# The MLP of a two-layer trunk in four quarters of 1024 hidden units in place of two halves

## What is computed

```
h   = layer_norm(ALPHA * h + mix, ...)
hid = square(relu(h @ mlp_w_up[layer] + mlp_b_up[layer]))        # 1024 -> 4096
h   = layer_norm(ALPHA * h + hid @ mlp_w_down[layer] + mlp_b_down[layer], ...)   # 4096 -> 1024
```

## Time and profile before

| | |
|---|---|
| Median of 3 runs | 1367.02 us (1365.03 to 1369.89) |
| The profiled execution | 1364.11 us, its span 1362.3 us |
| PE busy | 1312.8 us (96% of the span), granted clock 0.995 on average |
| DVE busy | 625.6 us (46%) |
| POOL busy | 515.8 us (38%) |
| ACT busy | 512.1 us (38%) |
| Moved by DMA | 108.27 MB, mean 79 GB/s, queue q1 with 141296 packets at 25.9% of 16 engines |

### The profile page before, as it was taken

One profiled execution on the slowest core, in us unless ns is written; L12 is line 12 of the kernel. 1 busy time (PEld: TensorE's weight loads), 2 busy tenths in 40 slices (PEclk: granted clock), 3 DMA queues, 4 the chain that ended last, 5 costly groups with the idle time before them and its releaser, 6 DMA issues.

```text
span 1362.3 us, 21811 instructions
## 1 busy us (share of the span) xinstructions
PE 1312.8 (96%) x9502; PEld 1178.8 (87%) x9502; DVE 625.6 (46%) x1052; ACT 512.1 (38%) x734; POOL 515.8 (38%) x220
## 2 busy tenths in 40 slices
PE   6999998999999999999999999999999999999996
PEld 5998855999999999999998988877788888888885
DVE  6999554456530024412356456465566300343125
ACT  4334487445222222222365245264453222223124
POOL 1001154355444444445544124114654444444440
PEclk9999999999999999999999999999999999999998
DMA  6221100222233322333221221212223333223321
GB/s 183 93 63 33 64 1 1 69 88 68 90 92 93 93 94 93 94 93 94 94 63 63 63 63 63 62 63 93 93 64 97 106 103 95 93 93 93 93 63 62
DMA packets 141791, 108.27 MB, mean 79 GB/s; under 512 B 8096, under 2 KB 139376, under 8 KB 141696
## 3 DMA queue, kind: packets, MB, share of 16 engines
q1 hardware_dynamic: 141296, 106.77, 25.9%
q10 hardware_dynamic: 400, 0.11, 0.0%
HBM read 104.77 MB, written 2.10 MB: 78 GB/s over the span
## 4 chain that ended last, share of the span: by engine, by line
PE 83%; ACT 7%; DVE 6%; issue 2%; DMA 1%; POOL 1%; SPq 0%; DVEq 0%; ACTq 0%
PE pb L706 63%; PE pb L872 2%; PE pb L718 2%; PE pb L873 2%; PE pb L874 2%; PE pb L812 1%; PE pb L813 1%; PE pb L750 1%; PE pb L811 1%; ACT wh L1289 1%; PE pb L1073 1%; DMA x_tok<-in_x 1%; DVE st L2313 1%; PE pb L982 1%; PE pb L1071 1%
## 5 line engine op out<-in xcount | busy, mean ns | idle before, releaser
L567 POOL TENSOR_TENSOR wl<-raw,wh 128x2048 fp32r<-128x2048 f32 x81 | 378.4, 4672 | 513.3 <-ACT wh L1289 513.1
L706 PE MATMUL pb<-hh,wh 128*128 128x264 f32 (+1 forms) x1160 | 301.6, 318 | 3.2 <-DVE qd L2295 1.6
L706 PE MATMUL pb<-hh,wl 128*128 128x264 f32 (+1 forms) x1160 | 296.9, 314 | 0.0
L706 PE MATMUL pb<-hl,wh 128*128 128x264 f32 (+1 forms) x1160 | 296.8, 314 | 0.0
L1289 ACT ACTIVATE wh<-raw 128x2048 fp32r<-128x2048 f32 x97 | 185.1, 1908 | 92.3 <-DMA raw<-in_mlp_w_down 62.2
L706 PEld LDWEIGHTS pb<-hh,wh 128*128 128x128 f32 x1160 | 190.7, 188 | 19.2 <-issue 3.7
L706 PEld LDWEIGHTS pb<-hl,wh 128*128 128x128 f32 x1160 | 190.6, 188 | 13.8 <-issue 1.2
L706 PEld LDWEIGHTS pb<-hh,wl 128*128 128x128 f32 x1160 | 190.5, 188 | 13.5
L706 PE MATMUL pb<-hidh,wh 128*128 128x264 f32 (+1 forms) x720 | 191.8, 321 | 0.0
L706 PE MATMUL pb<-hidh,wl 128*128 128x264 f32 (+1 forms) x720 | 191.0, 320 | 0.0
L706 PE MATMUL pb<-hidl,wh 128*128 128x264 f32 (+1 forms) x720 | 190.2, 318 | 0.0
(11 more groups left out here) (391 smaller groups left out, 2043.2 us busy)
## 6 DMA issues: line engine op xcount, KB each, us to landing
raw<-in_mlp_w_up SPq DMA_DIRECT2D x32, 1024.0 KB, 5.3
raw<-in_mlp_w_down SPq DMA_DIRECT2D x32, 1024.0 KB, 5.5
raw<-in_w_in_c SPq DMA_DIRECT2D x16, 1024.0 KB, 5.2
raw<-in_w_in_ab SPq DMA_DIRECT2D x8, 1024.0 KB, 5.5
raw<-in_w_out_ab SPq DMA_DIRECT2D x4, 1024.0 KB, 4.9
raw<-in_w_out_c SPq DMA_DIRECT2D x4, 1024.0 KB, 5.0
x_tok<-in_x SPq DMA_DIRECT2D x2, 1024.0 KB, 8.2
raw<-in_s_w_glu SPq DMA_DIRECT2D x1, 1024.0 KB, 5.4
```

The costliest lines, as they stand in the source:

```text
L567: pool.tensor_tensor(wl[:, c % RING, :], raw[:, c % RING, :], wh[:, c % RING, :].bitcast(F32), ALU.subtract).then_inc(w_lo, 1)
L706: mm = pe.matmul(pb[:, bank + b, 0:z_ - a], lhs, rhs[:, a:z_], start=first and hi and k == 0, stop=last and k == len(todo) - 1)
```

## The change

The MLP of each layer is cut in four quarters of 1024 hidden units: `up{l}q` and `down{l}q` with q = 0 to 3, each of 4 slots, 8 tiles, 8 chunks. The slots of the down stages now hold two tiles by 8 chunks, as all others of that size do. `down{l}0` is emptied as before (ACT with the bias, DVE with ALPHA*h), `down{l}3` by the layer norm. `down{l}1` and `down{l}2` are added to `h` by DVE straight from PSUM, one tensor_tensor a tile, and ACT has no part in them but the high parts of four slots, which in its program no longer wait for a tile. `hidh` and `hidl` become half as large. The matmuls are the same in number and size.

```
--- before.py
+++ after.py
@@ -42,9 +42,9 @@
     layer1 = [(f"{w}{p}", 1, n) for p in range(NPAIR) for w, n in (("f", 2), ("q", 2), ("i", NBLK))]
     for name, slots, tiles in [
         ("uqk", 6, 12), ("v", 2, 2 * NBLK), ("glu", 1, 4), ("out_ab", 4, 8),
-        ("up00", 8, 16), ("down00", 8, 8), ("up01", 8, 16), ("down01", 8, 8),
+        *[(f"{w}0{q}", 4, 8) for q in range(4) for w in ("up", "down")],
         *layer1, ("g", 4, 8), ("out_c", 4, 8),
-        ("up10", 8, 16), ("down10", 8, 8), ("up11", 8, 16), ("down11", 8, 8),
+        *[(f"{w}1{q}", 4, 8) for q in range(4) for w in ("up", "down")],
     ]:
         STAGES[name] = (slot, slots, tile, tiles)
         slot += slots
@@ -53,9 +53,9 @@
 
 
 NSLOTS = _plan()
-TOK = {"q0", "q1", "q2", "q3", "g", "out_c", "up10", "down10", "up11", "down11"}
-IN_TMP = ["glu", "up00", "down00", "up01", "up10", "down10", "up11"]
-LN_STAGE = ["out_ab", "down01", "out_c", "down11"]
+TOK = {"q0", "q1", "q2", "q3", "g", "out_c", *[f"{w}1{q}" for q in range(4) for w in ("up", "down")]}
+IN_TMP = ["glu", *[n for l in "01" for n in (f"up{l}0", f"down{l}0", f"up{l}1", f"up{l}2", f"up{l}3")]]
+LN_STAGE = ["out_ab", "down03", "out_c", "down13"]
 LOW_LN = {STAGES[name][0] + STAGES[name][1] + 2: n for n, name in enumerate(LN_STAGE[:3])}
 HALF_OUT = {0: 0, 2: 4}
 PIECES = {(0, 6): (0,), (0, 7): (1,), (1, 2): (2,), (1, 4): (3,)}
@@ -75,7 +75,7 @@
     count, table = {"act": 0, "dve": 0}, []
     for name, (_, _, _, tiles) in STAGES.items():
         for t in range(tiles):
-            by = "dve" if name == "glu" or name[0] in "fq" or name in LN_STAGE else "act"
+            by = "dve" if name == "glu" or name[0] in "fq" or name in LN_STAGE or name[:4] == "down" and name[5] in "12" else "act"
             count[by] += 1
             table.append((by, count[by]))
     return table
@@ -266,8 +266,8 @@
 
 
         m2 = ExitStack()
-        hidh = sb("hidh", [P, 16, LEAD + L], F32R, m2)[:, :, LEAD:]
-        hidl = sb("hidl", [P, 16, LEAD + L], F32R, m2)[:, :, LEAD:]
+        hidh = sb("hidh", [P, 8, LEAD + L], F32R, m2)[:, :, LEAD:]
+        hidl = sb("hidl", [P, 8, LEAD + L], F32R, m2)[:, :, LEAD:]
         rel = sb("rel", [P, 4, L], F32, m2)
         m2.close()
         m3 = ExitStack()
@@ -532,9 +532,9 @@
             stream("out_ab", w_out_ab[0], skip=2)
 
             def mlp(layer):
-                for half in range(2):
-                    stream(f"up{layer}{half}", mlp_w_up[layer], col0=2048 * half)
-                    stream(f"down{layer}{half}", mlp_w_down[layer][2048 * half:2048 * (half + 1), :], P, 16)
+                for q in range(4):
+                    stream(f"up{layer}{q}", mlp_w_up[layer], col0=1024 * q)
+                    stream(f"down{layer}{q}", mlp_w_down[layer][1024 * q:1024 * (q + 1), :])
 
             mlp(0)
             for p in range(NPAIR):
@@ -664,7 +664,7 @@
                                    ALU.subtract).then_inc(y_ready, 1)
             lows("glu")
             lows_ln(0)
-            for name in ["up00", "down00", "up01"]:
+            for name in ["up00", "down00", "up01", "down01", "up02", "down02", "up03"]:
                 lows(name)
             lows_ln(1)
             for p in range(NPAIR):
@@ -680,7 +680,7 @@
             for i in range(8):
                 out_low(i)
             lows_ln(2)
-            for name in ["up10", "down10", "up11"]:
+            for name in ["up10", "down10", "up11", "down11", "up12", "down12", "up13"]:
                 lows(name)
             lows_ln(3)
 
@@ -877,14 +877,14 @@
                             pieces(j * per + k)
 
             def mlp(layer, n):
-                for half in range(2):
-                    if half == 0:
+                for q in range(4):
+                    if q == 0:
                         run_after(n)
                     else:
-                        run(f"up{layer}1", hh, hl)
-                    seen = 16 * (2 * layer + half)
-                    run(f"down{layer}{half}", hidh, hidl, lambda k: (hid_ready, seen + k + 1), cols_=P, kcs=16,
-                        norm=2 * layer + 1 if half else None)
+                        run(f"up{layer}{q}", hh, hl)
+                    seen = 8 * (4 * layer + q)
+                    run(f"down{layer}{q}", hidh, hidl, lambda k: (hid_ready, seen + k + 1),
+                        norm=2 * layer + 1 if q == 3 else None)
 
 
             pe.wait_ge(consts, 3)
@@ -1271,9 +1271,9 @@
                         if kc % 4 == 3:
                             mm.then_inc(ot_done, 1)
                     if a == 0 and kc == 0:
-                        last_sum("down11", 3, 1)
+                        last_sum("down13", 3, 1)
                     if a == 0 and kc == 1:
-                        last_square("down11", 3, 1)
+                        last_square("down13", 3, 1)
 
 
         @block.scalar
@@ -1650,13 +1650,16 @@
             run_ln(0)
 
             def mlp(layer):
-                for half in range(2):
-                    c0 = 64 + 32 * layer + 16 * half
-                    run(f"up{layer}{half}", into_tmp(f"up{layer}{half}", ACT.Relu, lambda t: cols_a[:, c0 + t:c0 + t + 1]),
-                        None if half else lambda t, a: ahead_out(layer, t, a))
-                    if half == 0:
+                for q in range(4):
+                    c0 = 64 + 32 * layer + 8 * q
+                    run(f"up{layer}{q}", into_tmp(f"up{layer}{q}", ACT.Relu, lambda t: cols_a[:, c0 + t:c0 + t + 1]),
+                        None if q else lambda t, a: ahead_out(layer, t, a))
+                    if q == 0:
                         run(f"down{layer}0", into_tmp(f"down{layer}0", ACT.Identity,
                                                       lambda t: cols_b[:, 32 + 8 * layer + t:32 + 8 * layer + t + 1]))
+                    elif q < 3:
+                        for j in range(4):
+                            high(STAGES[f"down{layer}{q}"][0] + j + 2)
                 run_ln(2 * layer + 1)
 
             mlp(0)
@@ -2111,6 +2114,11 @@
 
                 _, _, t0, tiles = STAGES[name]
                 for t in range(tiles):
+                    if name[5] != "0":
+                        hc = cols(name, h[:, t, :])
+                        dve.wait_ge(tile_done, t0 + t + 1)
+                        TT(hc, hc, dense(name, t), ALU.add).then_inc(emptied_by["dve"], 1)
+                        continue
                     hm = flat(name, h[:, t, :])
                     wait_tile(name, t)
                     STT(hm, hm, ALPHA, flat(name, tmp[:, (t0 + t) % 2, :]), ALU.mult, ALU.add).then_inc(tmp_free, 1)
@@ -2224,7 +2232,7 @@
 
                 t0 = STAGES[name][2]
                 freed = 2 + tmp_before(name)
-                for t in range(16):
+                for t in range(8):
                     par = (t0 + t) % 2
                     a = flat(name, tmq[:, par, :])
                     r = flat(name, rel[:, t, :] if name[-1] == "0" and t < 4 else tmp[:, par, :])
@@ -2236,9 +2244,10 @@
                     TT(flat(name, hidl[:, t, :]), a, flat(name, hidh[:, t, :].bitcast(F32)), ALU.subtract).then_inc(hid_ready, 1)
 
             def mlp(layer):
-                hidden(f"up{layer}0")
-                residual(f"down{layer}0")
-                hidden(f"up{layer}1")
+                for q in range(3):
+                    hidden(f"up{layer}{q}")
+                    residual(f"down{layer}{q}")
+                hidden(f"up{layer}3")
                 layer_norm(2 * layer + 1, 1.0)
 
             layer_norm(0, ALPHA)
```

35 lines of the change are left out of this document (20 added, 15 removed).

## The result

| | before | after |
|---|---|---|
| Median | 1367.02 us (13 runs, 1364.1 to 1369.97) | 1370.3 us (13 runs, 1369.35 to 1375.38) |
| The profiled execution, its span | 1364.11, 1362.3 | 1369.84, 1367.9 |
| From norm 0's first add to the end of the span | 1070.8 | 1076.5 |

The ratio is 1.0031, with a 95% interval of 1.002 to 1.0043: slower by 0.3%, at the edge of what a measurement of this kernel can tell. The forecast was 1369.9 us. The two profiled executions stand 5.7 us apart, though, twice the 2.85 of the sum. The medians hide this, since the median of before lies 2.9 us above its profiled execution and that of after only 0.5 above its own. The lowest times, 1364.1 and 1369.35, are 5.25 apart. So the question for the experiments is what the sum left out.

The account below looks back on a forecast made before the run. PE's own matmul pace was taken as the bound, its work unchanged. Norm 1 +1.15, norm 3 +1.94 and pace -0.24 make +2.85 us, on the median of before 1369.9 us (+0.21%); range 1365.0 to 1377.0.

Parts of the forecast that it names:

- the sum: All terms together: norm 1 +1.15, norm 3 +1.94, pace -0.24, the rest 0, giving +2.85 us.
- Loads, high and low parts, evacuations at 0: Body of the MLP: loads, high and low parts and 16 added DVE adds per layer stay hidden behind PE, worth 0.
- Up to down at 0: Up-to-down turns, four a layer: slack before the last hidden chunk shrinks from 7.4 to 1.6 and 1.4 us; worth 0.
- POOL before `hidl`: Rival, end of up stages: POOL's low part blocks DVE, PE stalls 3.1 us a place, +25 for all; chance 0.10.
- Norm 1, +1.15: Norm 1: half 0 ends 2.88 us later, the chain gets 1.73 shorter through L2121 at 0.61; +1.15 us.
- Norm 3, +1.94: Norm 3, end of kernel: half 0 ends 2.80 us later, a 0.86 us wait for half 1 goes; +1.94 us.
- pace, -0.24: Layer 1's slow end behind the guess of the mean holds 60 matmuls less, at 4 ns each; -0.24 us.
- a fall behind norm 1: Rival: PE's clock falls behind norm 1 as behind norm 0, costing 1.33 us, 1371.2 us; chance 0.22.
- The chances: Odds given for the result against before: same 0.61, slower 0.35, faster 0.04, with 4.1 us (0.3%) as the bound.

Follow-up runs that it names:

- p_last16: The changed kernel with three parts a layer, of 8, 8 and 16 chunks, so the last stage is a half again; 1364.9 us, 0.9997 of before.
- a_race: The changed kernel with ACT's high part ahead of the ReLU at the last tile of every up stage; 1444.27 us, 1.0563 of before.
- b_race: The kernel before with ACT's high part ahead of the ReLU at the last tile of every up stage; 1372.33 us, ratio 1.0042.
- a_race_wait: As a_race, but in down1 and down2 of each layer ACT waits for the tile before each high part; 1434.91 us (one run).
- p_last8: The changed kernel with three parts a layer, of 16, 8 and 8 chunks, so the last stage stays short; 1370.26 us, 1.0031 of before.
- a_align: The changed kernel with a pad of 448 bytes a partition ahead of hidh, moving the rows of hidh and hidl; 1368.87 us, 1.0019 of before.
- b_fill: The kernel before with 12 matmuls that nothing needs in PE's gap behind norms 0, 1 and 2; 1364.73 us, ratio 0.9991.

## Why the prediction was right, and where it was not

**Loads, high and low parts, evacuations at 0:** right. No wait of PE in the body, and p_last16, which has all three, has the time of the kernel before.

**Up to down at 0:** right. The slack of 1.6 and 1.4 us held in all eight places. The rival's condition, POOL before `hidl`, never came, and its price, 3.1 us a place and 25 for eight, was not measured as it stands: a_race also puts ACT's high part ahead of the ReLU and so holds a square. With that, a place with one held instruction costs 3.6 to 3.8 us, and one with two 7.7 to 7.9, 50 us in all. What the prediction missed is the second hold: it counted one held instruction, but the freed highs let a second low part in behind the first.

**Norm 1, +1.15:** measured +1.40. The 24 matmuls less gave 2.96 for 2.88. The chain lost 1.56 of the 1.73 expected, with L2121 at 0.43 us and not 0.61, so its other steps gave a little back. The reason given for L2121 was roughly right, but the row says it more exactly: before, the second of the two lows, which begins late because its load comes late relative to half 0, ended at 674.71, 6.75 us behind the first add; after, the last one ends at 676.07, 5.15 behind it.

**Norm 3, +1.94, and pace, -0.24:** 1.70 together, measured 1.59.

**The clock, the term that was mis-sized.** In the sum it stood at 0, with a fall behind norm 1 as a rival at a chance of 0.22. It fell there (1.09 us), and it fell behind norm 2 as well (1.11 us), which the prediction named only as the place where a gap of 2.65 us cost nothing. That one row was taken as evidence against; it shows only that such a gap need not be followed by a fall. (The 0.35 us of its first matmul says little: behind norm 0, where the clock did fall, the first matmul took 0.36.) What brings it at norm 2 is open. It isn't dragged in by the fall behind norm 1, since b_race has the one without the other. In the profiles without filling, a gap of 2.65 us had no fall in two (before, p_last16) and one in the third (a_race_wait), and a gap of 2.41 or 2.42 had a fall in all five (after, p_last8, a_align, b_race, a_race), so the length of the gap doesn't decide it either. The third, the same line as the earlier trace rows and the window behind it:

```profile
1020.96 0.35 PE L812 MATMUL pb<-hh,wh 128*128 128x256 f32 x1 [2.65 <-ACT hh L1611]
```

```profile
1021.00:1025.20 4.20, 4.20 (x21) 4.08 (x22) 3.08 (x8) 2.10 (x6) 1.47 (x2) 0.59 0.23 81
```

The Trainium skill (TensorE: Matmul & The Clock Gate, part 1) says that how much runs slow varies from run to run; the profiled executions agree, since norm 2's code is the same with a fall and without.

**The sum, +2.85:** its own terms, norms 1 and 3 with the pace, measured 2.99. Another 0.42 came at and around norm 2, where the sum had nothing: 3.4 without falls. With them it is 5.6 in the profiles, so the sum has half of the difference between the profiled executions. That the median was forecast within 0.4 us is therefore partly luck and rests on which executions were profiled: the sum was laid on a median 2.9 us above its own profile.

**The chances:** with a fall behind norm 0 in every profile without filling and a gap of the same length coming at norm 1, the case of the clock there should have had over half, at +1.1 us. The result, +0.31%, lies on the bound between same and slower.

## What to carry to other kernels

Where a stage ends in a norm that is laid over its own last tile, the length of that tile's second half is the cover. Cutting the stage finer shortens the cover, and this is paid at once, and again in the clock when PE's gap grows from 0.8 to 2.1 us. Look at the last stage alone; the cut ahead of it was free here. A gap in PE that can't be closed can be filled with matmuls that nothing needs, if they are shorter than the gap: at norm 1 of b_fill, where the gap was 0.8 us, they cost 0.5. What was not tried: quarters in which two last tiles are computed half by half, to give the cover back with 8 chunks.

A step that is moved off a wait is also let loose. Ask what it can now run beside: here the high part, and behind it a low part that holds DVE for 4.6 us.
